# The delta rule of a four-layer model taken two channel blocks at a time instead of one

## The reference

```python
zs = z_rw + mu * (_time_shift(z_rw) - z_rw)
r, kr, vr, wl, al, gl = _split(zs, ...)
decay = jnp.exp(-jnp.exp(-jax.nn.softplus(-(w0 + jnp.tanh(wl) @ w2)) - 0.5))
iclr = jax.nn.sigmoid(a0 + al @ a2)
gate = jax.nn.sigmoid(gl) @ g2
kk = heads(kr * k_k); kk = kk / jnp.maximum(norm(kk), 1e-12)
kr = kr * (1.0 + (iclr - 1.0) * k_a)
# _rwkv7_scan, per head, state S of 64x64, over the tokens t:
#   S_t = S_{t-1} (diag(w_t) - kk_t^T (a_t * kk_t)) + v_t^T k_t ;  y_t = S_t r_t
y_rw = _head_norm(y_rw) * lnx_w + lnx_b
bonus = sum(rh * kh * r_k) * vh
out_rw = (y_rw + bonus) * gate
```

## Time and profile before

| | us |
|---|---|
| median of 3 runs (lowest, highest) | 2311.22 (2309.35, 2312.5) |
| the profiled execution, its own time | 2314.05 |
| its span in the trace | 2312.1 |
| PE busy | 2288.9 (99%) |
| VectorE busy | 1466.5 (63%) |
| ScalarE busy | 1105.7 (48%) |
| GpSimd busy | 205.1 (9%) |
| delta rule, from the first product of block 0 to the first turn of retention | 308.37 |

### The profile page before, as it was taken

One profiled execution on the slowest core, in us unless ns is written; L12 is line 12 of the kernel. 1 busy time (PEld: TensorE's weight loads), 2 busy tenths in 40 slices (PEclk: granted clock), 3 DMA queues, 4 the chain that ended last, 5 costly groups with the idle time before them and its releaser, 6 DMA issues.

```text
span 2312.1 us, 35491 instructions
## 1 busy us (share of the span) xinstructions
PE 2288.9 (99%) x13674; PEld 1919.8 (83%) x13674; DVE 1466.5 (63%) x1717; ACT 1105.7 (48%) x1399; POOL 205.1 (9%) x175
## 2 busy tenths in 40 slices
PE   8999999999999999999999999999999999999998
PEld 7887777788888888888888888888888888888887
DVE  5467888865575575565565567665754665665664
ACT  6455554445443443444444547855443443443443
POOL 0001142500010010010010001200100100100001
PEclk9999999999999999999999999999999999999999
DMA  8653434335666666656666665566666566666665
GB/s 278 186 169 96 114 113 115 108 131 196 181 187 199 191 183 200 190 178 205 190 184 192 186 187 182 158 200 185 181 197 192 180 201 193 188 192 194 189 191 171
DMA packets 217562, 413.62 MB, mean 179 GB/s; under 512 B 13329, under 2 KB 21905, under 8 KB 217297
## 3 DMA queue, kind: packets, MB, share of 16 engines
q1 hardware_dynamic: 215856, 409.00, 58.9%
q0 software_dynamic: 1424, 2.49, 0.4%
q10 hardware_dynamic: 144, 0.14, 0.0%
HBM read 409.48 MB, written 2.10 MB: 178 GB/s over the span
## 4 chain that ended last, share of the span: by engine, by line
PE 94%; DVE 3%; ACT 1%; DMA 1%; issue 1%; SPq 0%; DVEq 0%; ACTq 0%
PE acc_pair L244 19%; PE acc_pair L246 18%; PE acc_pair L245 18%; PE acc_pair L261 10%; PE tp_pair L261 10%; PE tp_pair L267 5%; PE acc_pair L267 5%; PE tp_pair L870 3%; PE acc_pair L870 1%; PE tp_pair L411 1%; DVE w_lo L233 1%; DMA raw<-in_ev_w_in 1%; PE tp_pair L1837 1%; PE acc_pair L1837 1%; PE tp_pair L1232 0%
## 5 line engine op out<-in xcount | busy, mean ns | idle before, releaser
L233 DVE TENSOR_TENSOR w_lo<-raw,w_hi 128x1024 fp32r<-128x1024 f32 (+1 forms) x760 | 1006.9, 1330 | 695.6 <-ACT w_hi L228 688.5
L228 ACT ACTIVATE w_hi<-raw 128x1024 fp32r<-128x1024 f32 (+1 forms) x760 | 800.9, 1055 | 898.8 <-PE acc_pair L246 574.3
L261 PE MATMUL acc_pair<-xT_both,w_hi 128*128 128x512 f32 x1024 | 317.9, 392 | 0.0
L261 PE MATMUL tp_pair<-xT_both,w_hi 128*128 128x512 f32 x1024 | 316.2, 390 | 0.0
L244 PE MATMUL acc_pair<-w_hi,xT_both 128*128 128x512 f32 (+1 forms) x736 | 295.7, 402 | 1.6 <-DVE w_lo L233 1.5
L246 PE MATMUL acc_pair<-w_hi,xT_both 128*128 128x512 f32 (+1 forms) x736 | 284.7, 387 | 0.0
L245 PE MATMUL acc_pair<-w_lo,xT_both 128*128 128x512 f32 (+1 forms) x736 | 284.3, 386 | 0.0
L244 PE MATMUL acc_pair<-w_hi,hidA_hi 128*128 128x512 f32 x640 | 249.8, 390 | 0.3 <-DVE w_lo L233 0.3
L246 PE MATMUL acc_pair<-w_hi,hidA_lo 128*128 128x512 f32 x640 | 249.0, 389 | 0.0
L245 PE MATMUL acc_pair<-w_lo,hidA_hi 128*128 128x512 f32 x640 | 249.0, 389 | 0.0
L244 PE MATMUL acc_pair<-w_hi,hidB_hi 128*128 128x512 f32 x624 | 244.0, 391 | 0.0
(11 more groups left out here) (292 smaller groups left out, 2315.5 us busy)
## 6 DMA issues: line engine op xcount, KB each, us to landing
raw<-in_ff_w SPq DMA_DIRECT2D x512, 512.0 KB, 4.2
raw<-in_ev_w_in SPq DMA_DIRECT2D x112, 512.0 KB, 3.7
raw<-in_od_w_in SPq DMA_DIRECT2D x64, 512.0 KB, 4.2
raw<-in_ev_w_out SPq DMA_DIRECT2D x32, 512.0 KB, 3.7
raw<-in_od_w_out SPq DMA_DIRECT2D x32, 512.0 KB, 4.0
raw<-in_ev_w_in SPq DMA_DIRECT2D x8, 288.0 KB, 4.7
z<-in_x_turned SPq DMA_DIRECT2D x4, 512.0 KB, 5.6
x<-in_x_in SPq DMA_DIRECT2D x4, 512.0 KB, 10.4
```

Of the source, the lines that this page charges most:

```text
L228: act.activation(w_hi[:, j % RING, :, 0:wide], raw[:, j % RING, :, 0:wide], ACT.Copy).then_inc(hi_ready, 1)
L233: dve.tensor_tensor(w_lo[:, j % RING, :, 0:wide], raw[:, j % RING, :, 0:wide], w_hi[:, j % RING, :, 0:wide], ALU.subtract).then_inc(lo_rea ...
L261: last = nc.tensor.matmul(o[:, :], w_hi[:, j % RING, kt % KU, c * P:(c + 1) * P], both, start=(kt == 0), stop=(kt == KT - 1))
```

## The change

Two blocks of channels (a "duo") are taken at a time:

- 4 duos in place of 8 blocks. Every elementwise operation is 128x512 where it was 128x256 (half as many), those whose constants are per channel stay 128x256. TensorE's small matmuls stay as many and as large; they come in groups of 16 where they came in groups of 8, and the ones sums are 512 columns wide at half the number.
- `more` is called with 8 parts after the tokens, 4 after the y matmuls, 2 after the w matmuls, with caps at 32 until level 5; a duo has 64 parts. In duo 0 it starts at part 8 (unit 2) and the budget counts from 4.
- The state chain runs once per duo, on two halves of the state.
- Moved between engines: the time shift is made by ScalarE (`act_shift`: the token before, times mu), VectorE's mix adds z times 1 - mu; the copy `inv_t` and the negation `u_neg` go from VectorE to ScalarE; the variance is read from PSUM by ScalarE's square root.
- Memory: the token matrices, `inv`, `inv_t`, `w_inv` and a square lie in x's memory, so x is loaded a second time (4 DMAs of 512 KB on SP's queue at unit 4 of retention's stage, after the last duo's output), and the output projection waits for it. `decay` lies in `junk`.
- v is centred straight from z (no copy v_in). TensorE waits for `a_ready` before the key and beta transposes, for z_ready 14 before duo 0's beta products.
- The first front is that of two blocks and starts earlier: VectorE's preparation and K, R mix at j=0, LoRA and key norm on TensorE at j=3 (j=6 before), tanh at j=4, decay at j=5, exp at j=6, root, reciprocal and beta at j=7.
- GpSimd does 24 rotation steps in each of duos 2 and 3, half of them behind its LoRA loads.

```diff
+DUO = 2
+DUOS, PAIRS, CHUNKS = RW_BLOCKS // DUO, DUO * NCHUNK // 2, DUO * NCHUNK
...
+        def act_shift(act, q, kinds):
+
+            for i in kinds:
+                block, t = mix_of(q, i)
+                act.activation(t[:, :, 0:1], z_at(q, block)[:, :, 0:1], ACT.Copy, scale=0.0).then_inc(sem("difference"), 1)
+                for g in range(DUO):
+                    act.activation(t[:, g, 1:T], z_of(q, block, g)[:, 0:T - 1], ACT.Copy,
+                                   scale=mu_of(block + DUO * q + g)).then_inc(sem("difference"), 1)
+
+        def dve_front_mix(dve, q, kinds):
+
+            for i in kinds:
...
+                dve.wait_ge(sem("difference"), 9 * q + 3 * i + 3)
+                for g in range(DUO):
+                    c = block + DUO * q + g
+                    dve.scalar_tensor_tensor(z_of(q, block, g), z_of(q, block, g), mu_rest[:, c:c + 1], t[:, g, :],
+                                             ALU.mult, ALU.add).then_inc(sem("mixed"), 1)
...
+            if p:
+                pool.wait_ge(sem("variance_done"), 2 * p)
                 load_gate_lora(pool, p)
-            if front:
+            if p < LAST - 1:
                 pool.wait_ge(sem("lora_done"), p + 2)
                 load_front_lora(pool, p + 2)
+            if turns is not None:
+                for i in range(12, 24):
+                    rotate_step(pool, turns + i // 6, i % 6)
...
+            split(2)
+            if front:
+                dve_front_mix(dve, q, (0, 1, 2))
+            split(3)
             for l in range(1, LEVELS):
                 dve.wait_ge(sem("y_done"), 5 * p + l)
-                dve.tensor_tensor(w_inv[:, :, :, :], over_items(CEYE, CHUNK), levels_turned, ALU.subtract).then_inc(sem("w_ready"), 1)
-                dve.wait_ge(sem("inv_t_done"), 5 * p + l)
-                dve.tensor_copy(inv_t[:, :, :, :], inverse_turned)\
-                   .then_inc(sem("inv_t_ready"), 1)
+                dve.tensor_tensor(w_inv[:, :, :, :], over_items(CEYE, CHUNK, 2, PAIRS), levels_turned, ALU.subtract)\
+                   .then_inc(sem("w_ready"), 1)
                 if l == 1:
+                    split(4)
...
+                if l == 4:
+                    split(8)
+                    if front:
+                        dve_front_rate(dve, front_own, q)
+                    if norm:
+                        dve_result_lo(dve, p - 1)
+                if l == 5:
+                    split(9)
+                    if front:
+                        dve_front_sum(dve, q)
+                    dve_bonus_lo(dve, p)
...
+            for i, (t, bank) in enumerate(((v_tok[:, :, :, :], v_turned), (kappa_tok[:, :, :, :], kappa_turned),
+                                           (key_tok[:, :, :, :], key_turned), (beta_tok, beta_turned))):
+                act.wait_ge(sem("tokens_done"), 4 * p + i + 1)
+                act.activation(t, bank, ACT.Copy).then_inc(sem("tokens_ready"), 1)
+            split(2)
+            if front:
+                act.wait_ge(sem("kappa_ready"), 4 * p + 4)
+                act_shift(act, q, (0, 1, 2))
+            split(3)
...
                         act_front_exp(act, q)
+                if l == 5:
+                    split(9)
+                act.wait_ge(sem("inv_done"), 5 * p + l)
+                act.activation(inv[:, :, :, :], levels, ACT.Copy).then_inc(sem("inv_ready"), 1)
+                if l == 2:
+                    split(6)
+                if l == 3:
+                    split(7)
+                    if norm:
+                        act_result_hi(act, p - 1)
+                    split(8)
+                if l == 4:
+                    evacuate(0)
+                    act_bonus_hi(act, p, front)
...
+        def more(pe, p, parts, m, cap=64):
+
+            due = max(parts[1], min(cap, parts[0] + m))
             for part in range(parts[1], due):
-                multiply_part(pe, RET_N + p, part, xT, 1)
-            parts[:] = due, max(due, parts[1])
+                group = DUO * p + part // 32
+                if part % 32 < 2 and group:
+                    pe.wait_ge(stg_written, 2 * (RET_STG + group) - 1 + part % 32)
+                multiply_part(pe, RET_N + group, part % 32, xT, 1)
+            parts[:] = min(cap, parts[0] + m), due
...
+                if l == 1 and front:
+                    pe.wait_ge(sem("rhs_ready"), p + 1)
+                    if norm:
+                        pe.wait_ge(sem("deviation_ready"), p)
+                    pe_front_lora(pe, p + 1)
+                more(pe, p, parts, 4, 32 if l < LEVELS - 1 else 64)
                 if l == 4 and front:
                     pe_front_sum(pe, p + 1)
                 pe.wait_ge(sem("w_ready"), 5 * p + l)
                 pe.wait_ge(sem("inv_t_ready"), 5 * p + l)
                 for h, b, a in items():
-                    to, w, x = levels[half(a), b, h, :], w_inv[half(h), a, b, :], inv_t[half(h), a, b, :]
-                    last = mm(to, x, w) if l < LEVELS - 1 else mm(to, w, x)
+                    to, w, t = levels[half(a), b, h, :], w_inv[half(h), a, b, :], inv_t[half(h), a, b, :]
+                    last = mm(to, t, w) if l < LEVELS - 1 else mm(to, w, t)
                 last.then_inc(sem("inv_done"), 1)
                 if l < LEVELS - 1:
-                    more(pe, p, parts, 1)
+                    more(pe, p, parts, 2, 32)
...
+            step_own(0).then_inc(sem("state_done"), 1)
+            out_own(0, 0)
+            out_own(1, 0).then_inc(sem("own_done"), 1)
             pe.wait_ge(sem("bonus_ready"), p + 1)
             step_own(1).then_inc(sem("own_done"), 1)
...
+            out_own(2, 0).then_inc(sem("own_done"), 1)
+            pe.wait_ge(sem("own_done"), 10 * p + 2)
+            step_own(2).then_inc(sem("own_done"), 1)
+            pe.wait_ge(sem("step_ready"), 2 * p + 2)
+            pe.wait_ge(sem("state_ready"), 6 * p + 2)
             step_state(1).then_inc(sem("state_done"), 1)
...
+                front_own = Chain(eng, "front_own")
                 if j == 0:
-                    once(eng, "masks_landed", 16)
                     rwkv_prepare_dve(eng)
+                    once(eng, "half_bias_ready", 4)
+                    dve_front_mix(eng, 0, (0, 1))
+                if j == 5:
+                    dve_front_decay(eng, front_own, 0)
+                    dve_front_sum(eng, 0, acc[2])
+                if j == 6:
+                    dve_front_rate(eng, front_own, 0)
+                    dve_front_mix(eng, 0, (2,))
+                if j == 7:
+                    split_lo(eng, RET_N, 0)
+                    dve_front_inverse(eng, front_own, 0)
+                    split_lo(eng, RET_N, 1)
+                    dve_front_beta(eng, front_own, 0)
+            elif role == "act":
+                if j == 0:
+                    act_shift(eng, 0, (0, 1))
+                if j == 1:
+                    rwkv_prepare_act(eng)
+                if j == 2:
+                    act_front_square(eng, 0)
+                if j == 4:
+                    act_front_tanh(eng, 0, acc[3], tp[0])
                 if j == 5:
                     once(eng, "z_ready", 12)
-                    dve_front_mix(eng, 0)
-                if j == 7:
-                    split_lo(eng, RET_N, 0)
-                    dve_front_mix(eng, 1, True)
-                    own = Own(eng, "front_own", 0, 7)
-                    dve_front_sum(eng, 0, acc[2])
-                    split_lo(eng, RET_N, 1)
-                    dve_front_decay(eng, own, 0)
-                    dve_front_key(eng, own, 0)
-                    split_lo(eng, RET_N, 2)
-                    dve_front_kk(eng, own, 0)
-            elif role == "act":
-                if j == 3:
-                    rwkv_prepare_act(eng)
+                    act_shift(eng, 0, (2,))
                 if j == 6:
-                    act_front_square(eng, 0)
-                    act_front_v(eng, 0)
+                    act_front_exp(eng, 0)
                 if j == 7:
                     split_hi(eng, RET_N, 0)
+                    act_front_root(eng, 0)
                     split_hi(eng, RET_N, 1)
-                    act_front_tanh(eng, 0, acc[3], acc[3][:, T:2 * T])
-                    split_hi(eng, RET_N, 2)
-                    act_front_exp(eng, 0)
-                    act_front_root(eng, 0)
             elif role == "pe":
-                if j == 6:
+                if j == 3:
                     once(eng, "masks_landed", 16)
                     once(eng, "lora_inputs", 5)
                     eng.wait_ge(stg_written, 12)
+                    pe_front_lora(eng, 0, acc[3], tp[0])
                     pe_front_sum(eng, 0, acc[2])
-                    pe_front_lora(eng, 0, acc[3])
 
         def head(role, eng):
...
+                def load_x(role, sp, j):
+                    if j == 4:
+                        once(sp, "out_done", DUOS)
+                        for k in range(4):
```

(10 more changed lines are left out.)

829 lines of the change are left out of this document (416 added, 413 removed).

## The result

The changed kernel takes 2327.72 us (median of 6 runs, 2325.22 to 2330.79) against 2311.73 for the kernel before (6 runs beside them): 1.0067 times, 95% interval 1.0056 to 1.0078. It is slower by 16 us. The forecast was 2306.5, faster, with a range that ended at 2316: wrong in sign and outside its range.

The account below looks back on a forecast made before the run. TensorE, busy 99%, was taken to bound the kernel. Terms -13.7 + 0.6 - 2.7 - 0.4 + 9.4 + 2.0 + 0.5 = -4.3 us gave 2306.9 against the median, stated as 2306.5; range 2297 to 2316.

Parts of the forecast that it names:

- term 1: TensorE leaves the projection for small groups 40 times in place of 80, 0.31 us saved each; together -13.7 us.
- The wait for the bonus sums: In each duo's tail, TensorE stands 1.6 us for bonus_lo; in the last duo 0.6 less, as it has no front.
- fill each other's waits: In the tail after the mixed products, two state-chain halves cover each other's waits: 6.0 us for both.
- term 2: Tail, last matmul ahead to second behind, less 0.45: 11.5 us against 11.2 for two before; +0.6 us in all.
- term 4: Start of the delta rule: first front serves two blocks, late steps and splits make TensorE wait; +9.4 us, bounds +3 and +14.
- z moves: Start of the delta rule: VectorE's moves ahead of the beta products take 1.28 us, half covered by the kappa group; +0.6 us.
- the missing parts at the cap: Duo 0, level 4: the budget hits 32, so parts that covered evacuations are missing; +0.8 us.
- term 5: GpSimd's rotations slow VectorE in levels 1 to 3 of duos 2 and 3; +2.0 us, bounds 0 and +8.
- the load of x: Retention's stage: second load of x, 4 DMAs, could make one unit late once; +0.5 us, bounds 0 and +4.
- - 2.7: Delta rule: TensorE's waits for inv_t and by_key go, with inv_t on ScalarE and more parts as cover; -2.7 us.
- - 0.4: Last duo: one front less to share; -0.4 us.
- Rival C: Levels: VectorE late beside GpSimd, w matmuls wait for w_inv; 10 us, 2317, slower; chance 0.20.

Follow-up runs that it names:

- the cut groups: Kernel with both edits, w matmuls of levels 1 to 4 cut into two groups of 8 with one part between, 16 visits more: 2308.98 us, ratio 0.9985.
- both edits: Changed kernel with duo 0's splits one unit earlier and two parts each ahead of the bonus-sums and rho_mixed waits: 2302.15 us, again 2302.81.
- the edited kernels: Changed kernel with duo 0's splits earlier, plus parts ahead of rho_mixed (2301.19 us), also bonus sums (2302.15), or one there and rhs_tok's copy earlier (2301.35).

## Why the prediction was wrong

**The visits (term 1, -13.7) held.** A visit costs 0.37 us by the rows and 0.33 by the cut groups, where 0.31 was taken. With both edits duos 1 and 2 take 74.4 and 75.3 us at full clock, where 74 to 75 was named. (The 12 x 0.1 of this term is 1.2, not 1.3, and the 6.4 less 4.7 of the tail is 1.7, not 1.6; nothing hangs on either.)

**The tail's size held, its make-up did not.** The wait for the bonus sums was there, 4.1 us in place of 5.8 (4 x 1.6, less 0.6). That the state chain's two halves "fill each other's waits" failed: VectorE makes own_states, two scaled and three rho_mixed ahead of what TensorE needs, and TensorE stood 1.54 us for it in every duo, 6.2 us. But the work around the waits was shorter than taken. Measured as in term 2, the four tails are 12.64, 12.77, 13.30 and 12.68 us, of which the clock took 4.8 (means of 0.90, 0.92, 0.88 and 0.94 over them): 46.6 at full clock, where 45.4 was forecast (4 x 11.5, less 0.6). The term is short by about 1 us, and that it came so close is in part luck.

**The start of the delta rule (term 4, +9.4) held in its first steps and was too short at its end.** From the transposes of the last group to the first product are 30.7 us (145.28 to 175.94) in place of 25.9: +4.8, where +4.7 was worked out; z moves 0.5 (0.6), unit 2 3.3 (3.3), the missing parts at the cap 0.8 (0.8). What was not seen is that in duo 0 every later split is one unit late too, since TensorE started a unit ahead: 1.5 us for one and 2.9 for unit 7, 4.4 that the sum had at nothing.

**GpSimd (term 5, +2.0) and the load of x (+0.5).** 1.7 us of waits for w_inv; no wait for x, and the waits from 480 us on are those of before. The retention stage is 1.3 us longer from its first turn to its first product with the scores, where the last variance and gate are now those of two blocks; the sum had that as equal work.

**The step that failed is the one that is not in the sum:** each wait was priced at its own length, and the clock at nothing. Of the windows the prediction read only that the clock was 1.00 before, and carried it over. It forecast the wait of 3.3 us at unit 2 and counted it as 3.3; in the kernel before, such a wait of 3.22 us cost 5.8. It forecast tails of 11.5 us without the projection in place of 5.6, and in all four tails the clock fell.

The account closes where the delta rule runs. The terms that act in this stretch are -13.7 + 0.6 - 2.7 - 0.4 + 4.7 + 2.0 = -9.5, so 298.9 us were forecast for it; 317.35 were measured, 18.5 more. Of these about 16 are the clock, 4.4 the later splits of duo 0 and 1 the tails; a visit worth 0.37 in place of 0.31 gives back 2.4 over 40 visits: 19 in all. At full clock and all else equal it would be about 301 us, 7 less than before. That the edited kernels run at 2301 to 2303, at the edge of the forecast's 2302 to 2311, does not confirm the sum: they also lack most of the 14 us of waits at unit 2 and in the tails, which the unedited kernel has. Rival C named the right sign for a reason that is worth 1.7 us of the loss; no rival was about the clock.

## What to carry to other kernels

A wait on TensorE costs more than its length where the clock falls with it. In this kernel, 99% busy, one new wait of 3.2 us cost 5.8; so price such a wait above its length, and look for windows with a clock under 1.00, not at the page's line of digits. As falls come and go between executions, look at more than one run's mean clock. Wider batches save visits and make the gaps between big matmuls longer: keep a few parts of the big work back and put them inside the long stretch of small matmuls, above all in its middle. When the first round of a loop starts ahead by one unit, everything that feeds it must start ahead too.

## What was not expected of the hardware

A stretch of 12.2 us of the tail's small matmuls, with no wait over 1.54 us in it, was enough for a fall to half clock that lasted until 4.5 us after the projection was taken up again (238.5 to 243.0); a stretch of 5.6 us was not. With 1.4 us of 128x512 matmuls ahead of rho_mixed the clock stayed at 1.00 in three of four duos. A wait of 3.22 us in the kernel before went with half clock for 3.4 us, from about 177.7, half a microsecond before the wait ended, to about 181.1. And one program fell to half clock at the start of duo 0 in one profiled execution and stayed at 1.00 in another.
